# Forming the sums of weight blocks on GpSimd instead of VectorE

## The reference, cut to what matters

```
def _swiglu(h, w_gu, w_down):          # D_MODEL 1024, D_FF 2816
    g, u = jnp.split(h @ w_gu, 2, axis=-1)
    return (jax.nn.silu(g) * u) @ w_down

for i in range(DEPTH):                 # DEPTH 2
    ...
    h = _rmsnorm(x, norm_ffn_g[i])
    x = x + _swiglu(h, ffn_w_gu[i], ffn_w_down[i])
```

## Time and profile before

| what | value |
|---|---|
| median of 3 runs | 1755.4 us (1754.39 to 1755.97) |
| profiled execution, its own time | 1752.71 us |
| its span | 1750.9 us |
| TensorE matmul busy | 1711.0 us, 98% |
| VectorE busy | 1164.7 us, 67% |
| ScalarE busy | 833.5 us, 48% |
| GpSimd busy | 229.7 us, 13% |
| first stretch of seven-product tiles | about 430 to 842 us |
| second stretch | about 1285 to 1698 us |

### The profile page before, as it was taken

One profiled execution on the slowest core, in us unless ns is written; L12 is line 12 of the kernel. 1 busy time (PEld: TensorE's weight loads), 2 busy tenths in 40 slices (PEclk: granted clock), 3 DMA queues, 4 the chain that ended last, 5 costly groups with the idle time before them and its releaser, 6 DMA issues.

```text
span 1750.9 us, 26390 instructions
## 1 busy us (share of the span) xinstructions
PE 1711.0 (98%) x10042; PEld 1668.6 (95%) x10042; DVE 1164.7 (67%) x2122; ACT 833.5 (48%) x1574; POOL 229.7 (13%) x253
## 2 busy tenths in 40 slices
PE   7999999999999999999999999999999999999998
PEld 6999888999999999999989999999999999999988
DVE  6142455458789898988461366632888888888865
ACT  5222455234455555555442346741445555555543
POOL 4000021360000000000230014425200000000003
PEclk9999999999999999999999999999999999999999
DMA  5320001501313131312232100041031222212121
GB/s 171 121 73 25 25 25 49 166 18 61 97 37 109 37 103 43 98 48 80 82 121 73 49 25 25 25 168 49 19 103 61 65 81 62 84 61 85 61 72 73
DMA packets 108940, 123.75 MB, mean 71 GB/s; under 512 B 4720, under 2 KB 105136, under 8 KB 108560
## 3 DMA queue, kind: packets, MB, share of 16 engines
q1 hardware_dynamic: 107760, 122.00, 21.3%
q10 hardware_dynamic: 1056, 0.07, 0.0%
HBM read 112.62 MB, written 9.44 MB: 70 GB/s over the span
## 4 chain that ended last, share of the span: by engine, by line
PE 80%; DVE 14%; ACT 2%; issue 2%; DMA 1%; POOL 0%; SPq 0%; DVEq 0%; ACTq 0%; POOLq 0%
PE bank L482 79%; DVE xT L1773 4%; DVE w_lo L1731 3%; DVE raw L1715 1%; DVE s_tmp L1718 1%; DVE qkv L1932 1%; DVE s_tmp L1712 1%; DVE w_lo L1689 1%; DVE xT L1950 1%; ACT w_hi L1116 1%; DMA raw<-in_mlstm_w_out_dram 0%; ACT u_five L1214 0%; DVE raw L1736 0%; DVE w_lo L1695 0%; DMA xs<-in_x_prompt_dram 0%
## 5 line engine op out<-in xcount | busy, mean ns | idle before, releaser
L482 PE MATMUL bank<-y_parts,w_hi 128*128 128x384 f32 x1920 | 497.6, 340 | 11.5 <-DVE w_lo L1689 10.4
L482 PE MATMUL bank<-h_hi,w_hi 128*128 128x384 f32 x1280 | 438.6, 343 | 4.5 <-DVE w_lo L1695 1.8
L482 PE MATMUL bank<-h_lo,w_hi 128*128 128x384 f32 x1280 | 432.2, 338 | 0.0
L482 PE MATMUL bank<-h_hi,w_lo 128*128 128x384 f32 x1280 | 431.9, 337 | 0.0
L482 PEld LDWEIGHTS bank<-y_parts,w_hi 128*128 128x128 f32 x1920 | 349.0, 189 | 15.9 <-DVE w_lo L1689 11.6
L482 PE MATMUL bank<-y_parts,w_lo 128*128 128x384 f32 x960 | 324.6, 338 | 0.0
L1158 ACT CAST w_hi<-raw 128x512 fp32r<-128x512 f32 (+1 forms) x360 | 188.9, 526 | 137.9 <-PE bank L482 137.6
L482 PEld LDWEIGHTS bank<-h_hi,w_hi 128*128 128x128 f32 x1280 | 240.6, 188 | 14.5 <-POOL h_lo L2480 3.5
L1731 DVE TENSOR_TENSOR w_lo<-raw,w_hi 128x512 fp32r<-128x512 f32 (+1 forms) x360 | 200.9, 567 | 63.0 <-ACT w_hi L1158 62.0
L482 PEld LDWEIGHTS bank<-h_lo,w_hi 128*128 128x128 f32 x1280 | 240.7, 188 | 1.2 <-issue 0.2
L482 PEld LDWEIGHTS bank<-h_hi,w_lo 128*128 128x128 f32 x1280 | 240.6, 188 | 0.6
(11 more groups left out here) (264 smaller groups left out, 2660.7 us busy)
## 6 DMA issues: line engine op xcount, KB each, us to landing
raw<-in_ffn_w_gu_dram SPq DMA_DIRECT2D x44, 1024.0 KB, 5.1
raw<-in_ffn_w_down_dram SPq DMA_DIRECT2D x40, 512.0 KB, 3.5
raw<-in_gla_w_in_dram SPq DMA_DIRECT2D x12, 1024.0 KB, 5.4
raw<-in_mlstm_w_in_dram SPq DMA_DIRECT2D x11, 1024.0 KB, 5.3
x_keep<-xT SPq DMA_DIRECT2D x2, 3072.0 KB, 10.7
xT<-x_keep SPq DMA_DIRECT2D x8, 768.0 KB, 6.6
raw<-in_mlstm_w_out_dram SPq DMA_DIRECT2D x4, 1024.0 KB, 7.1
raw<-in_gla_w_out_dram SPq DMA_DIRECT2D x4, 1024.0 KB, 6.2
```

The lines of the kernel that those rows point to most:

```text
L482: return nc.tensor.matmul(out, lhsT, rhs, start=start, stop=stop, skip_group_check=chained)
```

## The change

The three sums at the head of `fast_work` (and of `before_fast`, for the first tile of a layer) and the fourth inside `fast_low` go from VectorE to GpSimd. GpSimd makes them in a loop over the 36 tiles of a layer, behind the norm's `squares` and `norm_low`, with the same semaphores and the same waits. They no longer stand in VectorE's order, so a tile's first sum starts when the low part of unit 4 of the tile before is out (`op_lo`) and its weights have landed (`raw_loaded`). Nothing else changes.

```
--- before.py
+++ after.py
@@ -1699,25 +1699,6 @@
                 if s >= 4:
                     dve.wait_ge(lo_ready, s - 3)
 
-            def fast_sums(L, t):
-
-
-                kind, _, _ = FT[t]
-                u = NF * L + t
-                q, s = PAIRS * L + PFAST + t // 2, t % 2
-                nk = 2 if kind == "down" else 4
-                dve.wait_ge(raw_loaded[s], 16 * (q + 1))
-                if u:
-                    dve.wait_ge(op_lo, 6 * u - 1)
-                V.tensor_tensor(s_tmp0[:, 0:nk, :], w_block(s, 0, 0, nk), w_block(s, 1, 0, nk), ALU.subtract
-                                ).then_inc(op_sum, 1)
-                dve.wait_ge(op_sum, 4 * u + 1)
-                V.tensor_tensor(w_block(s, 1, 0, nk), w_block(s, 1, 0, nk), w_block(s, 1, 1, nk), ALU.add
-                                ).then_inc(op_sum, 1)
-                dve.wait_ge(op_sum, 4 * u + 2)
-                V.tensor_tensor(s_tmp1[:, 0:nk, :], w_block(s, 1, 0, nk), w_block(s, 0, 0, nk), ALU.subtract
-                                ).then_inc(op_sum, 1)
-
             def fast_low(L, t, j):
 
                 kind, _, _ = FT[t]
@@ -1730,11 +1711,6 @@
                     dve.wait_ge(w_hi_ready, 2 * q + s + 1)
                 V.tensor_tensor(unit(w_lo, j, nk), w_source(s, j, nk), unit(w_hi, j, nk).bitcast(F32), ALU.subtract
                                 ).then_inc(op_lo if j < 6 else w_lo_ready, 1)
-                if j == 1:
-                    dve.wait_ge(op_sum, 4 * u + 3)
-                    dve.wait_ge(op_lo, 6 * u + 1)
-                    V.tensor_tensor(w_block(s, 0, 0, nk), w_block(s, 0, 1, nk), s_tmp1[:, 0:nk, :], ALU.subtract
-                                    ).then_inc(op_sum, 1)
 
             def a_low(n, src, k, b, cols, L):
 
@@ -1776,8 +1752,6 @@
                     dve.wait_ge(s_act, gates - 2 + seen)
                     V.tensor_tensor(own[:, g, :], own[:, g, :], src, ALU.mult).then_inc(done, by)
 
-                if more:
-                    fast_sums(L, t + 1)
                 if opens:
                     dve.wait_ge(c_out, 3 * u)
                     dve.wait_ge(au_lo, n_unit + 2)
@@ -2412,7 +2386,6 @@
 
                     for g in range(4):
                         add_residual(q, 0, g, c + g % 2)
-                    fast_sums(L, 0)
                     fast_low(L, 0, 0)
                     fast_low(L, 0, 1)
                     for g in range(4):
@@ -2506,6 +2479,29 @@
                 if e < 4:
                     norm_low(e, 0)
 
+            def weight_sums(L, t):
+
+
+                kind, _, _ = FT[t]
+                u = NF * L + t
+                q, s = PAIRS * L + PFAST + t // 2, t % 2
+                nk = 2 if kind == "down" else 4
+                pool.wait_ge(raw_loaded[s], 16 * (q + 1))
+                if u:
+                    pool.wait_ge(op_lo, 6 * u - 1)
+                G.tensor_tensor(s_tmp0[:, 0:nk, :], w_block(s, 0, 0, nk), w_block(s, 1, 0, nk), ALU.subtract
+                                ).then_inc(op_sum, 1)
+                pool.wait_ge(op_sum, 4 * u + 1)
+                G.tensor_tensor(w_block(s, 1, 0, nk), w_block(s, 1, 0, nk), w_block(s, 1, 1, nk), ALU.add
+                                ).then_inc(op_sum, 1)
+                pool.wait_ge(op_sum, 4 * u + 2)
+                G.tensor_tensor(s_tmp1[:, 0:nk, :], w_block(s, 1, 0, nk), w_block(s, 0, 0, nk), ALU.subtract
+                                ).then_inc(op_sum, 1)
+                pool.wait_ge(op_sum, 4 * u + 3)
+                pool.wait_ge(op_lo, 6 * u + 1)
+                G.tensor_tensor(w_block(s, 0, 0, nk), w_block(s, 0, 1, nk), s_tmp1[:, 0:nk, :], ALU.subtract
+                                ).then_inc(op_sum, 1)
+
             def causal(ap, d, tiles, done):
 
                 sign = 1 if d == 0 else -1
@@ -2581,6 +2577,8 @@
                 q0 = PAIRS * L
                 (gla if L else mlstm)()
                 squares(q0 + POUT, 2 * L + 1)
+                for t in range(NF):
+                    weight_sums(L, t)
                 if L == 0:
 
                     pool.wait_ge(p_done, 6 * (NF - 1) + 1)
```

## The result

The changed kernel took 1761.7 us (median of 6 runs, 1759.3 to 1763.9), the kernel before 1754.8 us (6 runs, 1753.7 to 1756.0): a ratio of 1.0038, interval 1.0025 to 1.0051. The medians are 6.9 us apart, and the interval of the ratio stands for 4.4 to 8.9 us. That is slower by more than 0.2%. The forecast was 1757.7, within 1751.5 to 1774; the result lies 4.0 us above it.

The account below looks back on a forecast made before the run. TensorE, busy 98% of the span, was taken as the bound. Later third sums at eight places (+4.8 us) and the two stretch starts (-2.5) gave +2.3: 1755.4 becomes 1757.7 us, range 1751.5 to 1774.

Parts of the forecast that it names:

- my own case: Main forecast: later third sums cost 4.8 us, the starts give back 2.5; 1757.7 us, on its own 1753 to 1761, chance 0.5.
- The decisive place: Gate tile after four down tiles: third sum 0.6 us later, eight times, +4.8 us, bounds +1.6 and +7.
- my 0.53: TensorE's loss per eight-tile period in the kernel before, 88.23 less 87.70 us, all a faster VectorE could give back there.
- my 87.70: TensorE's time for the 504 matmuls a period of eight tiles needs, in us.
- the start: Start of each layer's stretch: TensorE's losses of 0.31 and 0.93 us go, 2 x 1.24 = -2.5 us, bound 0.
- The 0.31 us in front of tile 0: TensorE's loss while unit 0's low part stood behind tile 0's sums on VectorE; claimed to go.
- The 0.93 us at tile 1's sixth product: TensorE's loss at the start, where the cast waits for tile 1's sums; claimed to go, sums ending at 437.5 to 439.7.
- Down tiles bound by VectorE: Rival: the shared port makes down tiles cost VectorE 7.5 to 8.5 us; 1775 us at 8.0, 1790 at 8.5; chance 0.2.
- my tally: VectorE in a down tile: 5.9 + 4 x 0.45 = 7.7 us, less at least 0.4 hidden: 7.3, just TensorE's time.
- GpSimd slower on this shape: Rival: 128x512 sums take 1.5 us on GpSimd, +1.25 us at each of eight places, 1763 us; chance 0.2.
- Faster: Rival: 128x512 sums take 1.05 us or less, the eight stalls and the start go, -6.7 us, 1748.7; chance 0.1.
- the low parts with a second value: Sign: some of VectorE's low parts take 0.4 to 1 us above 0.68 in the profile after.

Follow-up runs that it names:

- gates_back: Changed kernel, but the sums of the eight gate tiles behind a run of down tiles go back to VectorE: 1755.7 us, ratio 0.9998 to the kernel before.
- gates_only: Changed kernel, but GpSimd makes only the sums of the eight gate tiles behind down tiles, VectorE all others: 1760.6 us, ratio 1.0028.
- gates_twice: Changed kernel with one more 128x512 subtraction on GpSimd ahead of sum 1 in the eight gate tiles behind down tiles: 1785.4 us, ratio 1.0171.
- pool_reorder: Changed kernel with the third sum made as B(1,1) minus sum 1, ahead of the in-place sum: 1748.6 us against 1755.3 before, ratio 0.9963.
- no_sums_port: Kernel before with one-element VectorE subtractions instead of sums, plus 288 GpSimd additions from constants that nobody waits for: 1787.3 us, ratio 1.0179.

## Why the prediction came out as it did

**The total.** The centre of the forecast, +2.3 us, was itself inside what I call no change, though I gave slower the largest chance (0.48). The medians moved by three times as much. The range of my own case, 1753 to 1761, was added up wrongly: the bounds of its terms, +1.6 - 2.5 and +7 - 0, give 1754.5 to 1762.4 on 1755.4. The result, 1761.7, is outside the first and inside the second.

**The decisive place: right, in place and in size.** I forecast +0.6 us at each of eight places behind the copy `u_five`. Measured: 0.53 to 0.58 in six of the eight rows of the table, 0.72 in one, 1.38 in one. That it is the chain of three sums, `gates_back` (it goes), `gates_only` (it alone remains), `gates_twice` (one more link, 1.67 us more distance) and `pool_reorder` (one link less, all of it gone and the stall of before too) show together. That stall was worth 88.23 - 87.81 = 0.42 us a period and not my 0.53, since the floor lies above my 87.70. A simple relation holds them: the period is 87.81 + (distance - 2.77) where the distance exceeds 2.77. It gives 88.23 from 3.19 (88.23 measured), 88.77 from 3.73 (88.77) and 89.56 from 4.52 (89.57). `gates_twice` departs from it by what the clock took.

**Inside that term two errors cancelled.** GpSimd's timeline at the place:

```profile
543.55 1.29 POOL L2492 TENSOR_TENSOR s_tmp<-raw 128x512 f32<-128x512 f32 x1 [3.75 <-DVE w_lo L1712]
...
544.92 1.36 POOL L2495 TENSOR_TENSOR raw<-raw 128x512 f32<-128x512 f32 x1
...
546.35 1.35 POOL L2498 TENSOR_TENSOR s_tmp<-raw 128x512 f32<-128x512 f32 x1
```

1.29 us for the 128x512 is the interpolated figure, 748 ns for the 128x256 the extrapolated 0.74. From the end of the low part of unit 4 to the third sum's end 4.3 us pass (543.40 to 547.70), the forecast's value without collision; I had added 0.35 for one (545.6 instead of 545.25). And that low part came 0.1 us earlier than before (0.66 us ahead of the copy `u_tmp`, against 541.92 - 541.37 = 0.55), not 0.4. Measured, the chain is 4.30 instead of 545.02 - 541.37 = 3.65 us, 0.65 more, less 0.11: the 0.54. That the forecast had 0.6 is in part luck. For the late low part VectorE's timeline has the reason:

```profile
539.11 1.10 DVE L1749 TENSOR_TENSOR xT<-xT,u_tmp 128x384 f32<-128x384 f32 x1
...
542.98 0.42 DVE L1712 TENSOR_TENSOR w_lo<-s_tmp,w_hi 128x256 fp32r<-128x256 f32 x1
...
545.51 3.35 DVE L1712 TENSOR_TENSOR w_lo<-raw,w_hi 128x256 fp32r<-128x256 f32 x3
...
548.78 1.65 DVE L1749 TENSOR_TENSOR xT<-xT,u_tmp 128x384 f32<-128x384 f32 x1
```

The addition at 539.11, which takes 0.55 us where nothing is in its way, stood behind the down tile's own fourth sum. I had taken the stretch from one low part to the next over from the trace of before, with no GpSimd in it.

**The term that was wrong: the start, forecast at -2.5 us, measured at -0.4.** The 0.31 us in front of tile 0 went in the main (0.2 per layer). The 0.93 us at tile 1's sixth product stayed, from the first copy to the ninth (101.45 against 101.42) and as TensorE's wait itself:

```profile
443.36 0.19 PEld L482 LDWEIGHTS bank<-h_hi,w_hi 128*128 128x128 f32 x1 [1.00 <-ACT u_five L1214]
```

I had let sum 1 begin some 2 us before 435.2 and allowed for a long VectorE instruction. It did begin early: at 436.16, 0.86 us after the first copy, where before the first sum came 437.96 - 433.20 = 4.76 after it. But the three took 2.67, 1.61 and 1.62 and ended at 442.23, 6.07 us after the first began, and the whole head start of 3.9 us was gone: the cast came 442.31 - 435.30 = 7.01 us after the copy, before 440.19 - 433.20 = 6.99. I had 4.3 to 4.8 us for the three and up to 1.7 more for one collision, so the 6.07 us lie within my 6.5. But I counted them from a start 0.9 us earlier, and took the whole 0.93 us as won although my latest end, 439.7, was already past the 439.3 that is in time. All three waited for VectorE, not one; with a collision at each and the later start nothing is gained at tile 1, and my bound of 0 was the value to take.

**The remainder.** +4.8 - 2.5 was the forecast; with the measured terms it is 8 x 0.55 + 0.8 - 0.4 + some 0.2, the +5.0 of the trace. The medians give 6.9 (4.4 to 8.9), which includes 5.0. The 0.8 is one late weight; the chain of waits has the DMA, and GpSimd's timeline the sum behind it:

```profile
715.53 6.00 DMA raw<-in_ffn_w_gu_dram
```

```profile
721.60 1.31 POOL L2492 TENSOR_TENSOR s_tmp<-raw 128x512 f32<-128x512 f32 x1 [4.27 <-DMA raw<-in_ffn_w_gu_dram]
```

This transfer took 6.0 us, where those of its kind take 5.1 in the median (4.9 to 5.8); with that it would have landed at 720.6, ahead of the low part of unit 4, which ended at 720.9 and otherwise releases the sum. On VectorE the sums began 1.5 us behind that low part, so such a landing would have been harmless. How often this happens in runs without a trace was not measured. What makes the difference between 5.0 and 6.9 is not shown; late weights and a clock that falls ahead of the stretch, as at 301 us, may each be a part of it.

**The rivals.** *Down tiles bound by VectorE* fell. Copies `u_tmp` of neighbouring down tiles start 7.31 us apart (536.75, 544.06), TensorE's own pace. The rows above give the hold: 1.65 instead of 0.55 us is 1.1 for a 128x512 sum, and 1.10 instead of 0.55 is 0.55 for a 128x256, near the forecast 1.0 and 0.45. The Trainium skill, "SBUF — State Buffer", section "Who interferes with whom", says that the port pair which the two engines share is an exclusive lock, and that the engine that comes second blocks until the first instruction is over. The trace agrees for an instruction that arrives while the other one runs: the one-element subtraction of `no_sums_port` ended 0.02 us behind the GpSimd addition. What a hold costs is thus what is left of the sum, 1.1 us in the longest of these rows. The 8.5 us per down tile did not come about, because not every sum holds VectorE so long. Of the four sums from 536.07 to 539.79 three hold an instruction, for 0.36, 0.54 and 0.55 us, 1.5 in all, where this rival had 4 x 0.64 and my tally 4 x 0.45; the other ran beside an addition from PSUM. In that down tile VectorE was busy for 7.17 of 7.31 us, and TensorE for all of them (the changed kernel's window):

```profile
536.75:544.06 7.31, 7.31 (x44) 7.31 (x43) 7.17 (x15) 4.36 (x11) 2.97 (x5) 1.00 0.43 143
```

*GpSimd slower on this shape* fell, with 1.29 to 1.36 us at the decisive place. *Faster* fell for the same reason, though `pool_reorder` is what it described: third sum in time, 6.7 us gained, on another mechanism.

**Signs.** Right: the period of 88.8 us, the place of the loss, the low parts with a second value (0.68 us alone and 1.78 in the timeline where they are held). Wrong: no gap at the start; chained sums 1.46 us apart (1.37 to 1.43 measured); and GpSimd's busy time rose by 350 us, not 250. My own durations give 160 x 1.29 + 128 x 0.74 = 301, so 50 of it was bad arithmetic; the rest is sums that were longer where they met VectorE's work.

## What to carry to other kernels

Before moving work off a busy engine, find the one instruction that the bound engine waits for, and count the links of the dependency chain in front of it: here 64 of 72 tiles could be moved for nothing, and the other eight cost 0.55 us each because three links became 1.37 us long instead of 0.7. Shortening the chain by algebra (three links to two) was worth 6.7 us against the kernel before with the slower engine, and beat every placement of the longer one that was tried. An engine whose instructions collide with another's at every link should be costed with a collision at each link, and its head start not be read from a trace in which it was idle.

## What was not expected of the hardware

- A VectorE subtraction of one element per partition, both inputs in SBUF, took 1.23 us beside a GpSimd 128x512 addition and 0.16 alone. A tiny instruction pays what is left of the other's length. A memset of the same element took 0.06 us in all 288 cases: with it the periods were 87.90 us, without it 90.2 where the granted clock stayed at 1.00, and 91.8 where it fell.
- Where GpSimd and VectorE both had work queued, they took turns: of the three low parts from 545.51 (one of 128x256, two of 128x512) the first two each waited for a sum, and the three took 3.35 us, where 0.42 + 1.28 = 1.7 would do by the earlier trace rows, while the sums stayed at 1.35. At the start of the stretch the sums were held as well, at 1.61 and 1.62 us.
- With a wait of 2.36 us, or up to 1.2 us behind it, the granted clock fell to 0.50 for about 3 us at all eight places of `gates_twice`. In `no_sums_port` it fell at eight of ten waits of 2.1 to 2.3 us, and after waits of 0.7 to 1.5 us in the changed kernel at none. A stall with such a fall cost about 1.4 us more than itself.
